# A hybrid block with routed experts: w1 in chunks of contiguous rows, gate and up computed chunk by chunk

## The chip, the core and the metric

The kernel runs on one core of a Trainium2 chip. The metric is the device time in microseconds of one execution; lower is better. Three runs of the kernel before stand beside one profiled execution of it. An engine's "row" below is a line of the profile or of an answer of its trace.

## What is computed

The input is `x` of 256 tokens by 1024 features, all in fp32. A first block does adaptive modulation, a mixer (dilated attention beside a gated delta rule) and a routed mixture of experts; two layers of a second block follow. The change touches the mixture of experts alone:

```python
N_EXPERTS, TOP_K, D_EXPERT, SWIGLU_LIMIT, SWIGLU_ALPHA = 32, 4, 1024, 7.0, 1.702

def clamped_swiglu(hgu):
    gate, up = jnp.split(hgu, 2, axis=-1)
    gate = jnp.minimum(gate, SWIGLU_LIMIT)
    up = jnp.clip(up, -SWIGLU_LIMIT, SWIGLU_LIMIT)
    return gate * jax.nn.sigmoid(SWIGLU_ALPHA * gate) * (up + 1)

h = modulate(x, norm2_w, shift2, scale2)      # rms_norm(x)*w*(1+scale)+shift
logits = h @ w_router + b_router              # top 4 of 32, softmax over the four
# for the tokens xb of expert e:
y = clamped_swiglu(xb @ w1[e] + b1[e]) @ w2[e] + b2[e]
# w1[e]: 1024 x 2048 (gate and up columns), w2[e]: 1024 x 1024
```

## The kernel before, in words

The program writes out each engine's order by hand. TensorE multiplies, VectorE and ScalarE work on what it leaves in the eight banks of its accumulator memory, GpSimd does little, and the sync engine (SP) issues nearly all transfers. Every step waits on counted semaphores.

**Expert pass.** Each expert is given 64 slots for tokens; tokens beyond 64 go to overflow blocks, of which this input has one. So there are 33 passes of one kind. A pass on TensorE is `step` (L1185): `up` (L1142), then `scatter` of the expert before, `gather` of the next one's tokens (L1122), `turn` (L1156, transposes of the activation), `gates` of the next, `down` (L1162). The token matrix of an expert is held as `xe`, features on partitions: 8 blocks of 128 features by 64 tokens. `halves` (L1135) issues one product of 64 tokens by 1024 columns as two matmuls of 512 columns into the lower and the upper 64 partitions of a bank; in fp32 each shows as two instructions in the trace. So one block of 128 weight rows by 1024 columns is four matmul rows of the profile.

`up` fills the gate bank GB and then the up bank UB. Each begins with the bias, a product of the expert's one-hot row (32 partitions) with the table of all biases (4 matmuls with K=32 in the trace), and goes on with 8 feature blocks (32 matmuls). Then VectorE runs `swiglu_v` (L962): clamp both, multiply, add one to the exponential that ScalarE made (L1040), reciprocal (L971), product (L973). The product is what `turn` waits for. `aT` holds its four transposes, and `down` multiplies them with w2.

**Weights.** The ring has six slots of 16 KB per partition. `expert_chunk` (L1231) cuts an expert into six chunks of 2 MB, one per slot. Chunks 0 and 1 are the gate columns of w1, feature rows 0 to 511 and 512 to 1023; 2 and 3 are the up columns; 4 and 5 are w2. Partition p of a chunk holds rows p, 128+p, 256+p and 384+p, each a contiguous run of 4 KB in the device's memory. In `later_sync` (L1240) the sync engine loops over experts 1 to 31: for each chunk it waits until its slot is free (`readers`, L1258: gate_f twice, up_f twice, y_f twice, the ends of gate, up and down of the expert before) and issues the transfer (L1268). Ahead of this loop it writes a table of relative-position rows to the device's memory (L1249) and reads it back (L1257). Expert 0 is loaded earlier, the overflow block by L1277.

**Modulation.** `modulate` (L394) computes h from x for both uses: per tile of 128 tokens one scale instruction over 1024 features (L401) and one shift instruction (L404). The second use stands ahead of the router (L898). `to_features` transposes h, the router matmul (L1074) uses the transposed h and the router weights `wrt`, and `gather` takes its columns from h in every pass.

## Time and profile before

| | |
|---|---|
| Device time, median of 3 runs | 2606.88 us |
| lowest and highest | 2591.89 and 2608.11 us |
| Span of the profiled execution, first to last instruction (the page gives no time of its own beside it) | 2597.9 us |
| TensorE busy | 2358.2 us, 91% |
| VectorE busy | 837.0 us, 32% |
| ScalarE busy | 333.9 us, 13% |
| Moved by the DMA engines | 603.41 MB, mean 232 GB/s |
| Mean granted TensorE clock | 0.931 of 2.4 GHz |

PE is TensorE's matmul stream, PEld its weight loads, DVE VectorE, ACT ScalarE, POOL GpSimd, SP the sync engine and SPq its DMA queue. The span is cut into 40 equal slices of 65 us in the page, where a digit is the busy share of a slice in tenths. `PEclk` is the clock that TensorE was granted, in tenths of the full 2.4 GHz; the lower level is 1.2 GHz. In a group of instructions the columns are busy time and the mean of one; behind the bar stands the idle time of the engine before them and what ended it.

### The profile page before, as it was taken

The numbers are of one execution on the slowest core, as the hardware profiler recorded it, in microseconds if no ns is written. First come the engines' busy times: TensorE is split into PE (matmuls) and PEld (weight loads), VectorE is DVE, ScalarE is ACT, GpSimd is POOL, SyncE is SP. The second block draws the span as 40 slices with busy tenths as digits, with TensorE's granted clock in tenths as the row PEclk, the third lists the DMA queues.
The fourth block names the chain that finished last, engine by engine and source line by source line (L and its number), as shares of the span: only waits on it lengthen the run. The fifth ranks groups of instructions, "written<-read, shape, count | busy, mean of one in ns | idle before, by whom it ended". The sixth has DMA issues, their size and how long they took to land.

```text
span 2597.9 us, 25146 instructions
## 1 busy us (share of the span) xinstructions
PE 2358.2 (91%) x10045; PEld 1253.4 (48%) x10045; DVE 837.0 (32%) x1274; ACT 333.9 (13%) x707; POOL 44.4 (2%) x25
## 2 busy tenths in 40 slices
PE   4988788999999999999999759989899899988999
PEld 2856442333333333333333235454786454546874
DVE  1454321222222222122222215551463045423550
ACT  1132100000000000000000011220221012211110
POOL 0001000000000000000000000000000001000000
PEclk8999878999898999999999869999999999989999
DMA  9463239999899999999999643423443333224431
GB/s 364 147 232 130 79 47 409 392 369 373 354 382 380 364 363 364 371 371 362 365 364 373 256 139 130 146 99 97 130 162 146 115 126 141 97 65 130 156 140 61
DMA packets 219468, 603.41 MB, mean 232 GB/s; under 512 B 10142, under 2 KB 66478, under 8 KB 219234
## 3 DMA queue, kind: packets, MB, share of 16 engines
q1 hardware_dynamic: 219394, 602.40, 62.1%
q8 instruction: 50, 0.82, 0.1%
q14 instruction: 24, 0.20, 0.0%
HBM read 599.23 MB, written 3.15 MB: 232 GB/s over the span
## 4 chain that ended last, share of the span: by engine, by line
issue 61%; PE 33%; DVE 3%; ACT 1%; POOL 1%; SPq 1%; DMA 1%; DVEq 0%; POOLq 0%
PE bank L560 16%; PE bank L568 7%; PE bank L1927 6%; PE bank L767 2%; PE bank L2158 1%; PE bank L552 1%; DMA normw<-in_norm_w_dram 1%; POOL arena L1443 0%; PE bank L434 0%; SPq L1962 0%; PE bank L1834 0%; DVE hbuf L1572 0%; DVE arena L1573 0%; DVE arena L2015 0%; DVE normw L2043 0%
## 5 line engine op out<-in xcount | busy, mean ns | idle before, releaser
L1138 PE MATMUL bank<-ring,arena 128*64 128x512 f32 x3168 | 760.1, 636 | 9.8 <-DMA ring<-in_w_dram 9.8
L1138 PEld LDWEIGHTS bank<-ring,arena 128*64 128x64 f32 x3168 | 231.8, 146 | 545.5 <-issue 532.3
L560 PE MATMUL bank<-hTbuf,ring 128*128 128x256 f32 x1856 | 405.7, 382 | 4.2 <-ACT hTbuf L1680 3.5
L560 PEld LDWEIGHTS bank<-hTbuf,ring 128*128 128x128 f32 x1856 | 355.0, 192 | 54.2 <-issue 5.5
L964 DVE TENSOR_SCALAR arena<-bank 128x512 f32<-128x512 f32 x33 | 22.8, 691 | 519.9 <-PE bank L1138 519.9
L1927 PE MATMUL bank<-ring 128*128 128x512 f32 x352 | 151.4, 592 | 0.0
L568 PE MATMUL bank<-ring,hTbuf 128*128 128x512 f32 (+2 forms) x384 | 151.2, 554 | 0.0
L1125 PEld LDWEIGHTS bank<-arena,hbuf 128*128 128x128 f32 x1056 | 123.8, 196 | 24.7 <-issue 24.6
L1138 PE MATMUL bank<-arena 32*64 32x512 f32 x396 | 121.7, 694 | 14.0 <-ACT arena L1044 14.0
L1125 PE MATMUL bank<-arena,hbuf 128*128 128x64 f32 x1056 | 128.0, 281 | 0.0
L957 DVE TENSOR_SCALAR arena<-con,arena 128x64 f32<-128x64 f32 x66 | 16.5, 250 | 320.7 <-PE bank L1138 307.0
L1642 DVE SCALAR_TENSOR_TENSOR arena<-bank,arena 128x254 f32<-128x254 f32 (+1 forms) x176 | 76.6, 477 | 127.7 <-ACT arena L1773 126.2
L1844 PE MATMUL bank<-ring,hTbuf 128*128 128x512 f32 x256 | 115.3, 604 | 0.0
L971 DVE RECIPROCAL arena<-arena 128x512 f32<-128x512 f32 x33 | 110.7, 3353 | 1.1
L568 PEld LDWEIGHTS bank<-ring,hTbuf 128*128 128x128 f32 x384 | 72.6, 190 | 75.1 <-issue 71.8
L1927 PEld LDWEIGHTS bank<-ring 128*128 128x128 f32 x352 | 66.9, 190 | 83.3 <-issue 83.2
L568 PE MATMUL bank<-ring,arena 128*128 128x512 f32 (+1 forms) x208 | 94.4, 614 | 10.0 <-ACT arena L1680 9.2
L1040 ACT ACTIVATE arena<-arena 128x512 f32<-128x512 f32 x33 | 20.8, 629 | 552.5 <-DVE arena L964 552.5
L552 PE MATMUL bank<-con,hbuf 128*128 128x128 f32 x128 | 25.7, 384 | 61.7 <-DVE hbuf L1457 41.0
L1844 PEld LDWEIGHTS bank<-ring,hTbuf 128*128 128x128 f32 x256 | 48.2, 193 | 62.5 <-issue 62.3
L1654 DVE RECIPROCAL arena<-arena 128x512 f32<-128x512 f32 x22 | 73.8, 3353 | 0.7
L1773 ACT ACTIVATE arena<-bank,arena 128x256 f32<-128x256 f32 x88 | 44.9, 560 | 212.8 <-PE bank L560 212.8
(342 smaller groups left out, 1705.7 us busy)
## 6 DMA issues: line engine op xcount, KB each, us to landing
ring<-in_w_dram SPq DMA_DIRECT2D x198, 2048.0 KB, 12.8
ring<-in_w_up_dram SPq DMA_DIRECT2D x44, 1024.0 KB, 6.5
ring<-in_w_in_dram SPq DMA_DIRECT2D x21, 2048.0 KB, 8.1
ring<-in_w_ada_dram SPq DMA_DIRECT2D x12, 2048.0 KB, 8.2
ring<-in_w_down_dram SPq DMA_DIRECT2D x10, 2048.0 KB, 7.7
ring<-in_w_out_dram SPq DMA_DIRECT2D x6, 2048.0 KB, 8.0
ring<-in_w_in_dram SPq DMA_DIRECT2D x4, 1024.0 KB, 13.4
ring<-in_w_proj_a_dram SPq DMA_DIRECT2D x2, 2048.0 KB, 7.9
```

The source lines that it names most:

```text
L552: ins = pe.transpose(B.bank(name, j)[:, at:at + P], src(k, tt), ident)
L560: ins = pe.matmul(B.bank(name, j)[:, i * T:(i + 1) * T], w[:, k, (first + i) * P:(first + i + 1) * P], hT[:, k, :], start=(k == 0), stop=( ...
L568: ins = pe.matmul(B.bank(name, j)[:, 0:width], xs(k), ws(k), start=(k == 0), stop=(k == kts - 1))
L767: return lambda out, u: pe.matmul(out, lhsT[:, u, :], rhs[:, u, :], start=True, stop=True)
L971: v.reciprocal(eb, eb).then_inc(F["s1"], 1)
L1125: ins = pe.matmul(XB[:, k * SLOTS:(k + 1) * SLOTS], h[:, tt, k * P:(k + 1) * P], psel[:, tt, :], start=(tt == 0), stop=(tt == 1))
L1138: ins = pe.matmul(bank[g * SLOTS:(g + 1) * SLOTS, :], lhsT, rhs[:, g * CH:(g + 1) * CH], start=start, stop=stop)
L1642: ins = v.scalar_tensor_tensor(out=y2[:, k, back:], in0=pb[:, k, 0:T - back], scalar=conv_cols[:, 44 * (2 - back) + m:44 * (2 - back) + m ...
L1654: then(v.reciprocal(fe[i % 2], fe[i % 2]))
L1773: ins = act.activation(split(y, 2)[:, k, :], pb[:, k, :], ACT.Identity, scale=conv_cols[:, 88 + m:89 + m], bias=conv_cols[:, 132 + m:133 + m])
L1844: pe.matmul(BL.bank(f"g{i}", tt)[:], hT[:, k, tt * P:(tt + 1) * P], w[:, k, :], start=(k == 0), stop=False)
L1927: ins = pe.matmul(BL.bank("dn", j)[:], actT[:, k, tt * P:(tt + 1) * P], w[:, k - 4 * i, half * CH:(half + 1) * CH], start=(k == 0), stop=( ...
```

## The change

Chunks 0 to 3 of an expert are now 256 whole rows of w1 each, gate and up columns together, and partition p of a chunk holds rows 2p and 2p+1, one contiguous run of 16 KB. The w2 chunks hold rows 4p to 4p+3 per partition, also 16 KB. To match, `modulate` in its second use writes h with the features of each group of 256 dealt in two: even ones first, then odd ones, four instructions of 256 features where one of 1024 was. The router weights are loaded in the same feature order. The activation product L973 reads its two inputs at every fourth column and writes contiguously, so that the transposes have the features on the partitions where the new w2 chunks expect them. `up` issues both biases first and then goes chunk by chunk: two feature blocks into the gate bank, the same two into the up bank. Three new semaphores c0, c1, c2 tell the sync engine that a chunk has been read; the fourth chunk is let go with `up_f`. The number of matmuls, their shapes and the bytes moved stay as they were.

```diff
--- before.py
+++ after.py
@@ -244,7 +244,7 @@
 MFLAGS = [
     "sel", "x_f", "xe",
     "pgt_f", "pgt",
-    "gate_f", "up_f",
+    "c0", "c1", "c2", "gate_f", "up_f",
     "g_in", "gu_out",
     "g_exp", "s1", "act",
     "at_f", "aT",
@@ -391,17 +391,30 @@
         def bview(b, n):
             return b[:].rearrange("p (a b) -> p a b", a=n)
 
-        def modulate(v, then, sh, nw, job, count):
+        def dealt(row):
+
+            return [row[:, 2 * P * c:2 * P * (c + 1)].rearrange("p (q k) -> p k q", k=2) for c in range(4)]
+
+        def held(row):
+            return [split(row[:, 2 * P * c:2 * P * (c + 1)], 2) for c in range(4)]
+
+        def whole(row):
+            return [row]
+
+        def modulate(v, then, sh, nw, job, count, deal=whole, held=whole):
 
             shift, scale = mod[:, 3 * sh * D:(3 * sh + 1) * D], mod[:, (3 * sh + 1) * D:(3 * sh + 2) * D]
             v.wait_ge(*B.taken(*job))
             then(v.scalar_tensor_tensor(out=scale, in0=scale, scalar=1.0, in1=normw[nw][:], op0=ALU.add, op1=ALU.mult))
             v.wait_ge(S["rs"], count)
             for tt in range(TT):
-                then(v.scalar_tensor_tensor(out=h[:, tt, :], in0=x[:, tt, :], scalar=rs[:, tt:tt + 1], in1=scale,
-                                            op0=ALU.mult, op1=ALU.mult))
+                for hp, xp, sp_ in zip(held(h[:, tt, :]), deal(x[:, tt, :]), deal(scale)):
+                    ins = v.scalar_tensor_tensor(out=hp, in0=xp, scalar=rs[:, tt:tt + 1], in1=sp_, op0=ALU.mult, op1=ALU.mult)
+                then(ins)
             for tt in range(TT):
-                v.tensor_tensor(h[:, tt, :], h[:, tt, :], shift, ALU.add).then_inc(S["h_new"], 1)
+                for hp, sp_ in zip(held(h[:, tt, :]), deal(shift)):
+                    ins = v.tensor_tensor(hp, hp, sp_, ALU.add)
+                ins.then_inc(S["h_new"], 1)
 
         def head(place):
 
@@ -895,7 +908,7 @@
             ins.then_inc(S["x_new"], 1)
             v.wait_ge(S["ss"], 2)
             v.tensor_scalar(ms, ss, 1.0 / D, EPS, ALU.mult, ALU.add).then_inc(S["ms"], 1)
-            modulate(v, then, 1, 1, ("ad2", 3), 2)
+            modulate(v, then, 1, 1, ("ad2", 3), 2, dealt, held)
 
             v.wait_ge(*B.ready("rt"))
             v.tensor_tensor(lg, split(B.bank("rt")[:, 0:2 * NE], 2), brt.unsqueeze(1).to_broadcast([P, 2, NE]), ALU.add)\
@@ -970,7 +983,8 @@
             v.wait_ge(F["s1"], 2 * n + 1)
             v.reciprocal(eb, eb).then_inc(F["s1"], 1)
             v.wait_ge(F["s1"], 2 * n + 2)
-            v.tensor_tensor(act_b, ub, eb, ALU.mult).then_inc(F["act"], 1)
+            v.tensor_tensor(act_b.rearrange("p (q a) -> p q a", q=4), ub.rearrange("p (a q) -> p q a", q=4),
+                            eb.rearrange("p (a q) -> p q a", q=4), ALU.mult).then_inc(F["act"], 1)
 
         def pgt_v(v, F, n, par):
             v.wait_ge(F["pgt_f"], n + 1)
@@ -1113,11 +1127,11 @@
 
             def weights(i, ch):
                 s = (N1 + ch) % RING
-                return slot(s).rearrange("p (k n) -> p k n", k=4), (slot_in[s], 16 * (per_slot[s] + 1) + 16 * i)
+                return split(slot(s), 2 if ch < 4 else 4), (slot_in[s], 16 * (per_slot[s] + 1) + 16 * i)
 
             def over_weights(j, ch):
                 s = (N1 + ch) % RING
-                return slot(s).rearrange("p (k n) -> p k n", k=4), (over_in[s], 16 + 16 * j)
+                return split(slot(s), 2 if ch < 4 else 4), (over_in[s], 16 + 16 * j)
 
             def gather(F, n):
                 for k in range(KT):
@@ -1144,14 +1158,18 @@
                 pe.wait_ge(F["sel"], n + 1)
                 if not (isinstance(n, int) and n == 0):
                     pe.wait_ge(F["gu_out"], n)
-                for m, (bank, flag) in enumerate(((GB, "gate_f"), (UB, "up_f"))):
+                for m, bank in enumerate((GB, UB)):
                     halves(bank, bsel[par], b12[:, m * D:(m + 1) * D], True, False)
-                    for a in range(2):
-                        w, landed = wts(i, 2 * m + a)
-                        pe.wait_ge(*landed)
-                        for k in range(4):
-                            ins = halves(bank, xe[:, 4 * a + k, :], w[:, k, :], False, a == 1 and k == 3)
-                    ins.then_inc(F[flag], 1)
+                for ch in range(4):
+                    w, landed = wts(i, ch)
+                    pe.wait_ge(*landed)
+                    for m, bank in enumerate((GB, UB)):
+                        for k in range(2):
+                            ins = halves(bank, xe[:, 2 * ch + k, :], w[:, k, m * D:(m + 1) * D], False, ch == 3 and k == 1)
+                        if ch == 3:
+                            ins.then_inc(F[("gate_f", "up_f")[m]], 1)
+                    if ch < 3:
+                        ins.then_inc(F[f"c{ch}"], 1)
 
             def turn(F, n):
                 pe.wait_ge(F["act"], n + 1)
@@ -1230,12 +1248,9 @@
 
         def expert_chunk(e, ch):
 
-            rows = slice((ch % 2) * CH, (ch % 2 + 1) * CH)
             if ch < 4:
-                src = A["w1"][0, e, rows, (ch // 2) * D:(ch // 2 + 1) * D]
-            else:
-                src = A["w2"][0, e, rows, :]
-            return src.rearrange("(k p) n -> p k n", p=P)
+                return A["w1"][0, e, 2 * P * ch:2 * P * (ch + 1), :].rearrange("(p k) n -> p (k n)", p=P)
+            return A["w2"][0, e, CH * (ch - 4):CH * (ch - 3), :].rearrange("(p k) n -> p (k n)", p=P)
 
         def later_sync(sp):
 
@@ -1255,11 +1270,11 @@
                     at = qt * 8 * P + odd * 4 * nk
                     src = bass.AP(scratch.tensor, odd * REL + T - 1 - P * qt, [[8 * REL - 1, P], [2 * REL, 4], [1, nk]])
                     sp.dma_start(split(biasbuf[:, at:at + 4 * nk], 4), src).then_inc(S["rel_in"], 16)
-            readers = ["gate_f", "gate_f", "up_f", "up_f", "y_f", "y_f"]
+            readers = ["c0", "c1", "c2", "up_f", "y_f", "y_f"]
 
             def views(ch):
                 s = (N1 + ch) % RING
-                return s, slot(s).rearrange("p (k n) -> p k n", k=4)
+                return s, slot(s)
 
             with sp.Fori(1, NE) as e:
                 for ch in range(RING):
@@ -1952,7 +1967,8 @@
                                        (alog, A["A_log"][0].partition_broadcast(P)),
                                        (dtb, A["dt_bias"][0].partition_broadcast(P)),
                                        (dnw, A["dn_norm_w"][0].partition_broadcast(P)),
-                                       (wrt, A["w_router"][0].rearrange("(k p) n -> p k n", p=P)),
+                                       (wrt.rearrange("p (c k) n -> p c (k n)", c=4),
+                                        A["w_router"][0].rearrange("(c p k) n -> p c (k n)", c=4, p=P)),
                                        (brt, A["b_router"][0].partition_broadcast(P)),
                                        (thin[0:32, 0:8], A["rel_bias_2"])):
                         sp.dma_start(dst2, src2).then_inc(S["small_in"], 16)
@@ -1964,7 +1980,7 @@
             for ch in range(RING):
                 n = N1 + ch
                 sp.wait_ge(*B.ready(*loads1[n - RING][2]))
-                sp.dma_start(slot(n % RING).rearrange("p (k n) -> p k n", k=4), expert_chunk(0, ch))\
+                sp.dma_start(slot(n % RING), expert_chunk(0, ch))\
                   .then_inc(slot_in[n % RING], 16)
             later_sync(sp)
 
```

## Rows read from the trace of the kernel before

**Rows 1.** From the page: span, busy share, and slices of TensorE, its clock and DMA.

```profile
span 2597.9 us, 25146 instructions
...
PE 2358.2 (91%) x10045; PEld 1253.4 (48%) x10045; DVE 837.0 (32%) x1274; ACT 333.9 (13%) x707; POOL 44.4 (2%) x25
...
PE   4988788999999999999999759989899899988999
...
PEclk8999878999898999999999869999999999989999
DMA  9463239999899999999999643423443333224431
```

**Rows 2.** Waits in the expert stage: who for whom, us in total, times, longest.

```profile
PE bank L1159 <- DVE arena L973: 42.2, 32, 6.7
...
PE bank L1138 <- DMA ring<-in_w_dram: 9.8, 3, 7.9
...
SPq L1268 <- PE bank L1138: 869.2, 85, 18.3
```

**Rows 3.** Windows, one pass each: length, busy by engine, PEclk, DMA share, GB/s.

```profile
521.95:554.05 32.10, 30.61 (x156) 12.18 (x154) 7.80 (x13) 2.42 (x4) 0.00 (x0) 1.00 0.99 390
554.05:589.51 35.46, 33.96 (x156) 12.80 (x154) 7.82 (x13) 2.42 (x5) 0.00 (x0) 0.90 0.90 355
589.51:624.53 35.02, 33.73 (x156) 12.90 (x154) 7.80 (x13) 2.42 (x5) 0.00 (x0) 0.90 0.92 360
727.11:760.92 33.81, 32.32 (x156) 12.58 (x154) 7.81 (x13) 2.42 (x4) 0.00 (x0) 0.95 0.95 373
897.31:932.19 34.88, 33.59 (x156) 13.12 (x154) 7.80 (x13) 2.42 (x5) 0.00 (x0) 0.90 0.91 360
932.19:965.99 33.80, 32.31 (x156) 12.53 (x154) 7.81 (x13) 2.42 (x5) 0.00 (x0) 0.95 0.95 372
```

**Rows 4.** Window over thirty passes, from the second exponential to the thirty-second.

```profile
417.67:1443.57 1025.90, 982.92 (x4622) 380.71 (x4620) 233.18 (x356) 72.61 (x120) 0.00 (x0) 0.93 0.94 372
```

**Rows 5.** Timeline of TensorE in one full-clock pass: start, us, what, idle before.

```profile
615.66 1.07 PE L1138 MATMUL bank<-arena 32*64 32x512 f32 x4
616.67 7.09 PE L1138 MATMUL bank<-ring,arena 128*64 128x512 f32 x32
623.68 1.99 PE L1177 MATMUL bank<-arena 64*128 64x512 f32 x8
625.60 3.79 PE L1125 MATMUL bank<-arena,hbuf 128*128 128x64 f32 x32
630.41 0.63 PE L1159 MATMUL bank<-con,arena 128*128 128x128 f32 x4 [1.03 <-DVE arena L973]
```

**Rows 6.** Timeline of VectorE in the same pass.

```profile
625.12 0.69 DVE L967 SCALAR_TENSOR_TENSOR arena<-arena 128x512 f32<-128x512 f32 x1
...
629.58 0.69 DVE L973 TENSOR_TENSOR arena<-arena 128x512 f32<-128x512 f32 x1
```

**Rows 7.** DMA in 618 to 638 us (expert chunks), in 25 to 29 us (constants).

```profile
DMA packets 2079, 8.25 MB, mean 413 GB/s; under 512 B 64, under 2 KB 64, under 8 KB 2079
...
DMA packets 216, 1.79 MB, mean 447 GB/s; under 512 B 16, under 2 KB 16, under 8 KB 93
```

**Rows 8.** Timeline of TensorE in expert 1.

```profile
397.88 8.77 PE L1138 MATMUL bank<-ring,arena 128*64 128x512 f32 x32 [7.92 <-DMA ring<-in_w_dram]
...
413.24 3.65 PE L1138 MATMUL bank<-ring,arena 128*64 128x512 f32 x16 [1.47 <-DMA ring<-in_w_dram]
```

**Rows 9.** Modulation before the router (timeline), and two-input instructions of 256 (groups).

```profile
315.51 1.28 DVE L401 SCALAR_TENSOR_TENSOR hbuf<-x,small,arena 128x1024 f32<-128x1024 f32 x1
316.83 2.36 DVE L404 TENSOR_TENSOR hbuf<-hbuf,arena 128x1024 f32<-128x1024 f32 x2
319.25 1.11 PE L552 MATMUL bank<-con,hbuf 128*128 128x128 f32 x4 [10.73 <-DVE hbuf L404]
...
L1492 DVE SCALAR_TENSOR_TENSOR arena<-arena 128x256 f32<-128x256 f32 x14 | 6.8, 485 | 0.7
```

**Rows 10.** Timeline of TensorE in the pass of 35.46 us: down, then gate.

```profile
562.85 9.84 PE L1138 MATMUL bank<-ring,arena 128*64 128x512 f32 x32
...
573.62 7.09 PE L1138 MATMUL bank<-ring,arena 128*64 128x512 f32 x32
```

## The prediction, made before the result was known

> **What bounds the kernel now.** I read the page's forty slices first [rows 1]. From slice 6 to 22 TensorE and the DMA engines are both at nine tenths: this is the expert stage, 33 passes (32 experts and one overflow block), where nearly the whole change lies. Two resources that full can't both be the bound, so the next view is the list of waits inside the stage [rows 2]. TensorE waited for weights three times, 9.8 us in all, while the sync queue waited 869.2 us for TensorE to let go of a ring slot. So the weights come early and TensorE sets the pace. Its one regular wait is the transpose at L1159, which waits 42.2 us in 32 times for the activation product at L973.
>
> The windows cut at the exponentials of successive experts [rows 3] show one pass. With the clock granted in full (1.00, 2.4 GHz) it takes 32.10 us; others take 33.80, 34.88, 35.02 and 35.46 at 0.95 or 0.90, which means that part of them ran at 1.2 GHz. Thirty passes took 1025.90 us, 34.20 each [rows 4]. So 2.1 us of every pass are clock. The last column matters too: at 32.10 us the transfers are at 0.99 of their capacity and 390 GB/s. The cover over the DMA is thin.
>
> The order inside a full-clock pass is in the rows of TensorE [rows 5] and VectorE [rows 6]: four bias matmuls, 32 with weights (gate), four bias, 32 (up), scatter of the expert before, gather of the next, a gap of 1.03 us, transposes, down. The gap ends when L973 ends.
>
> **The change, part by part.**
> (a) *Bias matmuls together, gate and up chunk by chunk.* The count of matmuls stays: 8 with K=32 and 64 with weights. What changes is how often TensorE goes from one kind to the other. From start to start, 4 bias matmuls take 616.67 - 615.66 = 1.01 us and 32 weight matmuls 623.68 - 616.67 = 7.01 us [rows 5]. With a pace u per matmul and an extra w per change of kind, 4u + w = 1.01 and 32u + w = 7.01, so u = 0.214 and w = 0.153 us. Two changes of kind fall away per pass: 2 x 0.153 = 0.31 us. New is that the accumulation goes between two banks, seven times more per pass. The scatter, 8 matmuls over four banks, takes 1.92 us against 8u + w = 1.87 [rows 5], so three bank changes cost at most 0.05 us; seven cost at most 0.12. I take 0.31 saved (bounds 0.19 and 0.31; zero if w belongs to the start of an accumulation and not to the change of kind). Over 33 passes: **-10.2 us**. All of it is on the path, since VectorE starts its chain only when the last up matmul is done.
>
> (b) *Three chunks released singly.* c0 is let go after about a quarter of the up work instead of half, c2 at three quarters instead of the end; c1 and the last chunk about where they were. The queue behind SP's wait is only the next chunks, and nobody on TensorE waits for them [rows 2]. Price 0, hidden by the lead of the transfers. If that cover were gone, the release would help.
>
> (c) *16 KB per partition.* 512 pieces of 4 KB become 128 of 16 KB per chunk. In a stretch of nothing but 4 KB pieces the queue moved 413 GB/s [rows 7]. The nearest row for larger ones is the start, where the constants come as 13 KB per partition: 447 GB/s over 4 us, a short window and so a rough figure. The gain is between none and 8 per cent of the transfer time, and it counts only where TensorE waits: expert 1, whose chunks are asked for late, behind the bias rows. There the last one gates the last 16 up matmuls at 413.24, 15.4 us after the first at 397.88 [rows 8]. I take 0.5 us (bounds 0 and 1.2): **-0.5**. That new weights come in the order in which they are used changes nothing here, since the last chunk still gates the end.
>
> (d) *The activation product with a stride.* L973 now reads both inputs at every fourth float. It lasts 0.69 us for 512 floats [rows 6] and TensorE waits for its end, so anything added counts in full, 33 times. No DVE row of this trace reads with such a stride. Below: 0, the same number of elements. Above: as if each float were fetched twice, the price of a two-input instruction of 1024, 2.36 / 2 = 1.18 us [rows 9], so +0.49 us, or +16 over all passes. I take 0, by the nearest row in size, type and place: L967 in the same pass, two fp32 inputs of 512, 0.69 us [rows 6]. I hold this loosely.
> The Trainium skill speaks against me: "SBUF — State Buffer", section "Door 1: The DMA port swizzle", says that memory is read in lines of 16 bytes, that full rate wants at least two hits on a line, and that each access which goes to a new line pays. Every fourth float is one hit per line. By that rule (d) costs about the upper bound, and the total comes out slower; no row here shows it. The stride of two in (e) keeps two hits.
>
> (e) *Modulation in four pieces.* Before routing, two scale instructions of 1.28 us and two shift instructions of 1.18 become four each of 256 floats; TensorE waits for the last of them at 319.25 [rows 9]. A two-input instruction of 256 lasts 0.485 us [rows 9]: 2 x (1.94 - 1.28) + 2 x (1.94 - 1.18) = +2.8 at most; as such instructions start before their predecessor's record ends, I take **+2.0**. Once.
>
> (f) Router weights in pieces of 256 bytes instead of 128, at the start, behind larger loads: 0.
>
> **Sum** with the clock as before: -10.2 - 0.5 + 2.0 = -8.7 us. The profiled span is 2597.9 us [rows 1], 9.0 below the median 2606.9 and inside the runs' 2591.9 to 2608.1; span after about 2589, and I apply the difference to the median: **2598 us**.
>
> **The rivals.**
> *R1, the strided product costs.* Place: L973, price up to 0.49 us a pass. It decides from 0.26 us on (8.7 / 33): above that the kernel is slower than before. With the full price and the clock as before: -8.7 + 16.2 = +7.5, 2614 us. The longer trough before down is where the clock falls: in the pass of 35.46 us the 32 weight matmuls of down take 9.84 us, in the gate behind it 7.09 again [rows 10]. If no pass ran at full clock any more and the mean were 35.02 instead of 34.20, 31 x 0.8 = 25 more (without the first and the last pass): 2640 us. For it: nothing hides behind L973. Against it: no row.
>
> *R2, the clock gives it back.* Three different sequences of passes come to one mean: 32.10, 35.46, 35.02 to 34.19; with a 33.81 added to 34.10; 34.88, 33.80, 33.81 to 34.16 [rows 3]. The 32.10 is paid for by the 35.46 behind it. It looks as if the clock's stretches set the mean and not the sum of the work, and then 0.31 us saved turn into a longer stretch at 1.2 GHz. Result: -0.5 + 2.0 + a little, 2608 us, no change.
>
> *R3, the clock gives more.* The same shift may go the other way: the pass is shorter by 0.31 us and more of the troughs go by at full clock. If the mean came to 33.6 instead of 34.20: 31 x 0.6 = 19, with (e): 2589 us; if to 33.3, 2580.
>
> *R4, the DMA becomes the bound.* A pass moves 6 x 2.1 = 12.6 MB; at 34.20 us that is 368 GB/s. If 16 KB pieces ran 20 per cent below 413 [rows 7], at 330 GB/s, a pass would take 38.1 us: 31 x 3.9 = +121, 2728 us. It decides from 11 per cent down. Against it: the 13 KB pieces are not slower. That the change doesn't do what it says (the pieces still move as 4 KB) only takes away the 0.5 of (c).
>
> **Chances.** Forecast (0.31 kept, product free) 0.35; R2 0.20; R3 0.15; R1 0.25, of which 0.10 with the clock lost too; R4 0.05. The sign is thus open between small numbers; what lies outside 1 per cent (26 us, about what a measurement of this kernel tells from no change) is R3's far end, 0.10, and R1 with the clock or R4, 0.15. Range: 2578 (R3 with a little more) to 2636 (R1 with most of its clock). The forecast's own range is 2588 to 2606.
>
> **What would show it.** Step (a): from the first bias matmul to the scatter 15.7 us at full clock instead of 16.0 (2 x 1.01 + 2 x 7.01). (d): the duration of the product, 0.69 or 1.2, and the gap before the transposes, 1.0 or 1.5. (c): no wait of TensorE for weights after expert 1, and the rate in a stretch of expert loads at 413 or above. (e): 2 us more between the mean squares and the first transposes. R2, R3: the mean of thirty passes, 34.2 against 33.9 (forecast) or below, and how many are at clock 1.00. The prediction is wrong if the product lasts over 0.95 us, if a full-clock pass isn't 31.8 us, or if the mean pass moves by over 0.6 us while the full-clock pass doesn't.

## The result, and the profile after

The changed kernel takes 2619.62 us (median of 10 runs, 2612.44 to 2624.59) against 2607.35 us before (10 runs, 2591.89 to 2612.46): ratio 1.0055, 95% interval 1.0035 to 1.0075. It is a little slower. The prediction had it a little faster, 2598 us; the range of 2578 to 2636 holds the measured time, the direction was wrong.

The page of the changed kernel: the head, sections 1 and 2.

```profile
span 2612.7 us, 25156 instructions
...
PE 2362.8 (90%) x10043; PEld 1269.3 (49%) x10045; DVE 850.6 (33%) x1286; ACT 334.1 (13%) x707; POOL 44.4 (2%) x25
...
PEclk9989868899999999989999869989999999989999
DMA  9463239888888998888888543423443334224431
```

Beside [rows 1] the slices of DMA in the expert stage went from 9 to 8: the same bytes with less time of the engines. VectorE is busy for 13.6 us more. TensorE's clock has one nine less, 30 instead of 31, and one of the lost ones stands behind the experts (the 27th slice).

The waits of TensorE and of the sync queue in 380 to 1510 us, as in [rows 2]:

```profile
PE bank L1177 <- DVE arena L986: 54.1, 32, 7.0
...
PE bank L1152 <- DMA ring<-in_w_dram: 6.8, 3, 4.4
```

```profile
SPq L1283 <- PE bank L1152: 942.1, 151, 20.2
```

The wait for the product (L986 now, L973 before) grew from 42.2 to 54.1 us in 32 times, which is the 0.37 us of the next rows. They stand in a pass of the changed kernel whose trough ran at full clock, TensorE and then VectorE, to be laid beside [rows 5, 6]:

```profile
592.37 3.79 PE L1139 MATMUL bank<-arena,hbuf 128*128 128x64 f32 x32
597.56 0.63 PE L1177 MATMUL bank<-con,arena 128*128 128x128 f32 x4 [1.40 <-DVE arena L986]
...
608.59 1.93 PE L1152 MATMUL bank<-arena 32*64 32x512 f32 x8
```

```profile
L986 DVE TENSOR_TENSOR arena<-arena 128x512 f32<-128x512 f32 x33 | 35.1, 1064 | 1.1
```

The same group in the kernel before:

```profile
L973 DVE TENSOR_TENSOR arena<-arena 128x512 f32<-128x512 f32 x33 | 22.8, 692 | 1.1
```

The product lasts 1.06 us where it lasted 0.69, and the gap before the transposes is 1.40 us where it was 1.03. The reader should see the two 0.37 us as one: nothing hides behind this instruction. The eight bias matmuls now stand together and take 1.86 us to the next start.

Windows of the changed kernel: thirty passes, then three kinds of pass (columns as in [rows 3]).

```profile
418.21:1448.20 1029.99, 976.26 (x4622) 387.50 (x4620) 244.41 (x356) 72.62 (x120) 0.00 (x0) 0.93 0.89 370
557.41:591.30 33.89, 32.02 (x156) 12.76 (x154) 8.19 (x13) 2.42 (x5) 0.00 (x0) 0.95 0.89 371
625.18:660.02 34.84, 33.18 (x156) 13.23 (x154) 8.17 (x13) 2.42 (x4) 0.00 (x0) 0.90 0.87 361
1069.15:1105.57 36.42, 34.76 (x156) 13.58 (x154) 8.18 (x13) 2.42 (x4) 0.00 (x0) 0.86 0.83 346
```

No pass of the thirty ran at full clock; before, four of them did, at 32.1 us as the first of [rows 3]. There is a new kind at clock 0.86, 36.42 us. The mean is 34.33 us against 34.20 [rows 4]. So the expert stage lost little in this execution. More went behind it, where no instruction was changed. From the last exponential of the stage to the end, before and after:

```profile
1487.56:1687.56 200.00, 160.80 (x532) 88.08 (x532) 82.51 (x163) 37.50 (x86) 13.25 (x5) 0.88 0.39 133
1687.56:1851.56 164.00, 144.26 (x528) 85.83 (x527) 59.91 (x60) 32.20 (x87) 0.69 (x1) 0.95 0.32 106
1851.56:2597.90 746.34, 704.97 (x2560) 468.12 (x2558) 304.79 (x457) 117.20 (x262) 13.24 (x5) 0.96 0.36 122
```

```profile
1493.76:2612.70 1118.94, 1017.79 (x3615) 648.62 (x3616) 447.58 (x678) 187.05 (x435) 27.19 (x11) 0.94 0.35 121
```

The three windows of before add up to 1110.34 us; the one of after is 1118.94 us, 8.6 us more, with VectorE and ScalarE as busy as before (447.2 and 447.6 us, 186.9 and 187.1) and TensorE busy 7.8 us longer for the same matmuls: 1017.79 against 1010.04. That is its clock: cut into the same three lengths, the stretch of after has a granted clock of 0.87, 0.90 and 0.96 against 0.88, 0.95 and 0.96, and in the second TensorE gets through 496 matmuls where it did 528.

### The profile page after: what moved, and what is told of

The parts are those of the page before. It is cut to its first block, busy times and chain, and to the rows that moved or that the text cites. A ratio compares the mean times of both kernels' runs of the same rounds, so it can differ in the third digit from the quotient of the medians.

```text
span 2612.7 us, 25156 instructions
## 1 busy us (share of the span) xinstructions
PE 2362.8 (90%) x10043; PEld 1269.3 (49%) x10045; DVE 850.6 (33%) x1286; ACT 334.1 (13%) x707; POOL 44.4 (2%) x25
## 4 chain that ended last, share of the span: by engine, by line
issue 61%; PE 33%; DVE 3%; ACT 1%; DMA 1%; POOL 1%; SPq 0%; DVEq 0%; POOLq 0%
PE bank L573 15%; PE bank L581 7%; PE bank L1942 6%; PE bank L780 2%; PE bank L2174 1%; PE bank L565 1%; DMA ring<-in_w_ada_dram 1%; POOL arena L1458 0%; PE bank L447 0%; PE bank L434 0%; PE bank L1849 0%; DVE hbuf L1587 0%; DVE arena L1588 0%; DVE arena L2031 0%; DVE normw L2059 0%
## 5 line engine op out<-in xcount | busy, mean ns | idle before, releaser
L1152 PE MATMUL bank<-arena 32*64 32x512 f32 x396 | 114.8, 687 | 13.4 <-ACT arena L1058 13.4
L1177 PE MATMUL bank<-con,arena 128*128 128x128 f32 x132 | 26.5, 336 | 57.3 <-DVE arena L986 57.3
```

The costliest lines, as they stand in the source:

```text
L1152: ins = pe.matmul(bank[g * SLOTS:(g + 1) * SLOTS, :], lhsT, rhs[:, g * CH:(g + 1) * CH], start=start, stop=stop)
L1177: ins = pe.transpose(YB[:, q * P:(q + 1) * P], act_b[:, q * P:(q + 1) * P], ident)
```

## The experiments

In all of them a pass is counted from one exponential to the next, and "thirty passes" from the second to the thirty-second, as in [rows 4]. Each ratio is to the kernel before as it ran beside that experiment. The **work of a pass** is the time that it takes with the clock at 1.00 throughout.

### Taking the parts away

**e1: w2 and the product as before, all else as changed.**

```diff
-            v.tensor_tensor(act_b.rearrange("p (q a) -> p q a", q=4), ub.rearrange("p (a q) -> p q a", q=4),
-                            eb.rearrange("p (a q) -> p q a", q=4), ALU.mult).then_inc(F["act"], 1)
+            v.tensor_tensor(act_b, ub, eb, ALU.mult).then_inc(F["act"], 1)
-            return A["w2"][0, e, CH * (ch - 4):CH * (ch - 3), :].rearrange("(p k) n -> p (k n)", p=P)
+            return A["w2"][0, e, CH * (ch - 4):CH * (ch - 3), :].rearrange("(k p) n -> p k n", p=P)
```

> The changed kernel with w2 fetched as before (four 4 KB rows per partition) and the product reading contiguously again; w1 in 16 KB, chunk order, biases first and single releases stay. Theory P (the strided read is what made it slower): the product lasts 0.69 us again instead of 1.07, a full-clock pass takes 31.8 us, and the kernel is no slower than before. If the work saved counts, the mean pass is 33.8 to 33.9 us and the ratio to before 0.995 to 0.997; if the clock sets the mean (theory C), the mean pass stays at 34.1 to 34.2 and the ratio is 1.000. Rival D (the 16 KB pieces or the chunk order cost something): ratio stays at 1.005 with the product at 0.69.

Measured: ratio 0.9996 (0.9976 to 1.0015). The product lasts 0.692 us, six of the thirty passes ran at full clock in 31.81 us, and the mean is 33.70:

```profile
L986 DVE TENSOR_TENSOR arena<-arena 128x512 f32<-128x512 f32 x33 | 22.8, 692 | 1.1
```

```profile
418.82:1429.80 1010.98, 968.44 (x4622) 386.45 (x4620) 233.22 (x356) 72.61 (x120) 0.00 (x0) 0.94 0.92 377
1474.58:2586.51 1111.93, 1011.20 (x3616) 642.41 (x3616) 447.15 (x678) 186.96 (x435) 27.19 (x11) 0.95 0.36 121
```

Rival D falls: w1 in 16 KB runs, the chunk order and the single releases cost nothing that shows. What made the changed kernel slower came in with w2's layout and its product. This run takes both back at once, and no run has w2 in 16 KB runs with a contiguous product; but in the changed kernel TensorE never waits for weights after expert 1 (420 to 1450 us), so w2's loads are not what it waits for. The two readings of the clock are not told apart by this run: the profiled execution has the lower mean of theory W, the median of the runs gained nothing. That execution, at 2588.7 us, was one of the quickest of the twelve. What became of the saved work shows when the twelve are laid beside their granted clocks ("The clock over the kernels" below).

**e2: the kernel before, both biases first, nothing else.**

```diff
-                for m, (bank, flag) in enumerate(((GB, "gate_f"), (UB, "up_f"))):
+                for m, bank in enumerate((GB, UB)):
                     halves(bank, bsel[par], b12[:, m * D:(m + 1) * D], True, False)
+                for m, (bank, flag) in enumerate(((GB, "gate_f"), (UB, "up_f"))):
```

> The kernel before with one edit: both biases ahead of the gate matmuls. Full-clock pass 31.8 us instead of 32.1 if the 0.15 us per change of kind is real (32.1 if it belongs to the start of an accumulation). Theory W (work counts): mean pass 33.9, ratio 0.996. Theory C (the clock gives it back): mean pass 34.1 to 34.2, ratio 1.000, and another mixture of passes.

Measured: ratio 0.9972 (0.9945 to 0.9999). TensorE in a pass at full clock, and the windows of thirty passes and of one such pass:

```profile
908.68 1.93 PE L1138 MATMUL bank<-arena 32*64 32x512 f32 x8
910.54 13.95 PE L1138 MATMUL bank<-ring,arena 128*64 128x512 f32 x64
924.43 1.99 PE L1178 MATMUL bank<-arena 64*128 64x512 f32 x8
```

```profile
420.33:1432.86 1012.53, 969.98 (x4622) 386.23 (x4620) 233.15 (x356) 72.62 (x121) 0.00 (x0) 0.94 0.96 376
960.42:992.23 31.81, 30.31 (x156) 12.35 (x154) 7.81 (x13) 2.42 (x4) 0.00 (x0) 1.00 1.00 394
```

From the first bias matmul to the scatter 924.43 - 908.68 = 15.75 us, where the kernel before takes 2 x (623.68 - 615.66) = 16.04 [rows 5]. The 0.15 us per change of kind are real. In this profile the mean pass fell by more than the work, from 34.20 to 33.75 us, but the stretch behind the experts took 1119.0 us instead of 1110.3. Over all executions the median fell by 5.3 us (2594.07 against 2599.37) where 33 x 0.30 = 9.9 us of work were saved, and the interval of the ratio just excludes no change. So the work counts here, but the clock didn't give more than was saved.

**e3: the kernel before, with w2 in 16 KB runs and the strided product.**

```diff
-            v.tensor_tensor(act_b, ub, eb, ALU.mult).then_inc(F["act"], 1)
+            v.tensor_tensor(act_b.rearrange("p (q a) -> p q a", q=4), ub.rearrange("p (a q) -> p q a", q=4),
+                            eb.rearrange("p (a q) -> p q a", q=4), ALU.mult).then_inc(F["act"], 1)
-                src = A["w2"][0, e, rows, :]
+                return A["w2"][0, e, rows, :].rearrange("(p k) n -> p (k n)", p=P)
```

> The kernel before with w2 in 16 KB runs and the strided product; gate and up as before. Theory P: product 1.07 us, gap before the transposes 1.4 us, a full-clock pass would be 32.5 us. If work counts: mean pass 34.6, ratio 1.005. If the longer gap also costs clock: no pass at full clock, mean 34.9 or more, ratio 1.008 or more. If the clock alone sets the mean: 34.2, ratio 1.000.

Measured: ratio 1.0003 (0.9979 to 1.0026). The product lasts 1.07 us as in the changed kernel, and yet the time doesn't change:

```profile
L973 DVE TENSOR_TENSOR arena<-arena 128x512 f32<-128x512 f32 x33 | 35.2, 1067 | 1.1
```

```profile
416.87:1442.17 1025.30, 969.41 (x4622) 375.99 (x4620) 244.47 (x356) 72.60 (x120) 0.00 (x0) 0.95 0.93 371
1486.20:2589.50 1103.30, 1002.38 (x3616) 634.97 (x3616) 447.50 (x678) 186.86 (x435) 27.19 (x11) 0.96 0.36 122
930.17:964.31 34.14, 32.27 (x156) 12.52 (x154) 8.19 (x13) 2.42 (x5) 0.00 (x0) 0.95 0.93 368
```

Every pass of the thirty but the first took 34.1 to 34.2 us, all at clock 0.95, and the thirty are 34.18 in the mean, where 0.37 us more work on 34.20 would be 34.6. This is rival R2 with its sign turned: 0.37 us of work were added and the clock gave them back. The product isn't free here: the twelve executions had a mean granted clock of 0.938 where the kernel before had 0.931, and at one clock e3 is the slower of the two ("The clock over the kernels").

**e4: the changed kernel, reading contiguously and writing with the stride.**

```diff
-            v.tensor_tensor(act_b.rearrange("p (q a) -> p q a", q=4), ub.rearrange("p (a q) -> p q a", q=4),
-                            eb.rearrange("p (a q) -> p q a", q=4), ALU.mult).then_inc(F["act"], 1)
+            v.tensor_tensor(act_b.rearrange("p (q a) -> p a q", q=4), ub.rearrange("p (a q) -> p a q", q=4),
+                            eb.rearrange("p (a q) -> p a q", q=4), ALU.mult).then_inc(F["act"], 1)
```

> The changed kernel, but the product reads contiguously and writes with the stride (each next float 512 bytes on). If only reads by lines cost, the product lasts 0.69 us and this equals e1 in time with all weights in 16 KB runs. If a strided write costs as a strided read, 1.07 us and ratio 1.005 to before; if each write of a new line costs more, over 1.2 us and ratio 1.01.

Measured: ratio 1.0041 (1.0019 to 1.0063); the product lasts 1.041 us.

```profile
L986 DVE TENSOR_TENSOR arena<-arena 128x512 f32<-128x512 f32 x33 | 34.4, 1041 | 1.1
```

A strided write costs nearly what a strided read costs. There is no free side to put this stride on.

**i1: one strided input instead of two** (the other is read contiguously, so its columns no longer match and the activation is another one).

```diff
-            v.tensor_tensor(act_b.rearrange("p (q a) -> p q a", q=4), ub.rearrange("p (a q) -> p q a", q=4),
+            v.tensor_tensor(act_b.rearrange("p (q a) -> p q a", q=4), split(ub, 4),
                             eb.rearrange("p (a q) -> p q a", q=4), ALU.mult).then_inc(F["act"], 1)
```

> The changed kernel, the product reading only the exponential's input with the stride and the other contiguously (the columns then don't match, so the activation is another one). Both inputs strided took 1.07 us, none 0.69. If the cost is per strided stream and they add up: 0.88. If one strided stream already sets the pace of the instruction: 1.07.

Measured in its one execution: 1.070 us, as with two.

```profile
L986 DVE TENSOR_TENSOR arena<-arena 128x512 f32<-128x512 f32 x33 | 35.3, 1070 | 1.1
```

One strided stream sets the pace of the instruction. What in the stride costs is not shown: no run gives this instruction a stride of two or three floats.

**i2: the changed kernel, slots released in pairs.**

```diff
-            readers = ["c0", "c1", "c2", "up_f", "y_f", "y_f"]
+            readers = ["c1", "c1", "up_f", "up_f", "y_f", "y_f"]
```

> The changed kernel with the slots of w1 released in pairs again: chunks 0 and 1 after the second chunk, 2 and 3 at the end of up. Everything else as changed. Forecast step (b) priced the single release at nothing: ratio 1.005 as the changed kernel, no wait for weights after expert 1. If the single release had a price or a use: ratio off by more than 0.003 from the changed kernel's.

Measured: ratio 1.0094 (1.0068 to 1.0120), 0.0039 above the changed kernel's first ratio and 0.0046 above its second (g0 below), whose intervals it meets only at the edge. Yet in 420 to 1450 us TensorE waited for weights once, 1.2 us, and its thirty passes took 1040.60 us, 34.69 each, inside what the changed kernel itself shows (34.33 and 34.78). By the mark set above, a change of over 0.003, the release has a use. But it isn't a wait for weights, and at one granted clock i2 takes what the changed kernel takes ("The clock over the kernels"): its executions ran at a lower clock, 0.9205 in the mean against 0.9224. Why they did stays open.

### What repeats and what does not

**g0: the changed kernel once more**, unedited.

> The changed kernel once more, to see what repeats. Up to the last exponential of the expert stage it is 6 us behind the kernel before, and another 8.5 us are lost behind the expert stage, where no instruction was changed (1118.8 instead of 1110.3 us), in stretches at 1.2 GHz around the attention of the first layer. Theory H (the expert stage hands the layers a fixed place in the clock's rhythm): the stretch behind the last exponential is again 1118 to 1119 us. Rival N (chance of the single execution): it is anywhere between 1103 and 1119.

Measured: ratio 1.0048 (1.0027 to 1.0070).

```profile
420.00:1463.50 1043.50, 990.95 (x4622) 390.90 (x4620) 244.48 (x356) 72.63 (x121) 0.00 (x0) 0.91 0.88 365
1509.10:2628.10 1119.00, 1017.93 (x3615) 648.36 (x3616) 447.62 (x679) 187.05 (x435) 27.19 (x11) 0.94 0.35 121
```

The thirty passes are 13.5 us longer than in the first profile, with five passes at 36.4 us instead of one; the stretch behind them is the same to 0.1 us. This profile is of the slowest of g0's ten executions, 2630.31 us where their median is 2615.98.

**h0: the kernel before once more**, unedited.

> The kernel before once more, for a second profile of it. Theory H (the expert stage hands the layers a place in the clock's rhythm, and in the changed kernel always the same bad one): behind the last exponential 1110 us again or another value below 1118. Rival N: 1118 to 1119 is seen here too. The thirty passes should come to 34.1 to 34.3 us each.

Measured: one run, 2589.93 us.

```profile
417.50:1439.70 1022.20, 978.76 (x4622) 378.55 (x4620) 233.28 (x357) 72.66 (x121) 0.00 (x0) 0.94 0.95 373
1483.90:2588.10 1104.20, 1003.32 (x3615) 636.56 (x3616) 447.28 (x678) 186.98 (x435) 27.19 (x11) 0.96 0.36 122
```

Thirty passes at 34.07, and 1104.20 us behind them. Before thus shows 1110.3 and 1104.2 us there, the changed kernel 1118.9 and 1119.0 (and i2 1118.8). e2, which has neither the strided product nor a larger run, shows 1119.0 too; e3 shows 1103.3. The other kernels lie between: f4, f6 and e4 at 1118.7 to 1119.0, i1 at 1116.4, f3 at 1115.7, e1 at 1111.9. So the two profiles of the changed kernel lose 9 to 15 us there, but the loss is not peculiar to one of its parts, and i1, which differs from it in one input of the product, shows 2.5 us less. That it hangs on how the expert stage leaves TensorE's clock is the likely reading and isn't shown. Nor is the place fixed for the kernel before: 69 of its executions have spans from 2585.9 to 2613.5 us, and 20 of the changed kernel from 2605.2 to 2628.1.

**g1: the changed kernel with an idle instruction between the experts and the layers.**

```diff
+            then(v.reciprocal(t[:, 0:256], t[:, 0:256]))
             for tt in range(TT):
...
```

> The changed kernel with one idle reciprocal of 256 columns (1.7 us) on the path between the experts and the layers. It adds 1.7 us of work. Theory H: the layers start at another place in the clock's rhythm, the stretch from the last exponential to the end falls from 1118.8 to about 1105 to 1112 in spite of the added work, and the median is 5 to 10 us lower than the changed kernel's (ratio to before 0.999 to 1.003). Rival N: 1.7 us slower than the changed kernel, ratio 1.006.

Measured: ratio 1.0060 (1.0037 to 1.0083). In the profile the last stretch fell as theory H has it, in spite of the 1.7 us added:

```profile
1497.17:2609.89 1112.72, 1009.82 (x3615) 643.59 (x3616) 449.33 (x679) 187.20 (x435) 27.21 (x11) 0.95 0.36 121
```

The median did not fall. Either the other five executions left the experts at another place, or the gain was lost elsewhere; only one was profiled. Theory H is borne out by one profile, and the gain in time that it foretold did not come.

### Filling the gap

In the changed kernel TensorE idles 1.40 us behind each gather. The bias matmuls of the next expert need nothing that isn't there by then: both banks have been read by the clamps. The edit moves them, for three bases.

```diff
                 if more:
                     gather(M, i + 1)
+                if more:
+                    biases(M, i + 1, 1 - par)
                 if not first:
                     pe.wait_ge(M["ysb"], i)
                 turn(M, i)
```

**f4: on the changed kernel.**

> The changed kernel with the two biases of the next expert issued in the gap before the transposes (behind the gather), all weights in 16 KB runs, strided product. TensorE's gap of 1.4 us is filled, the pass at full clock would be 30.9 us. With the gap filled the strided product (1.07 us) costs nothing. If work counts: mean pass 31.5 to 32.9, 1.3 to 2.7 us less than 34.2, ratio 0.970 to 0.985. If the transfers become the bound: 12.6 MB a pass at 431 GB/s is 29.2 us, so not with 16 KB runs. If the clock alone sets the mean: 34.1, ratio 1.00.

**f3: on e1** (contiguous product).

> As the one before, but w2 in four 4 KB rows and the product contiguous (0.69 us). The bias matmuls fill the gap either way, so the strided product should make no difference: full-clock pass 30.9 us as well. Against the one before it tells the product on the path (no difference expected) from the transfers: w2 at 413 GB/s instead of 431 makes a pass of transfers 29.7 us, still below 30.9, so the same time within 0.1 per cent; slower if the DMA is now the bound.

**f6: on the kernel before.**

> The kernel before (weights in 4 KB rows, gate then up, contiguous product) with the two biases of the next expert issued in the gap behind the gather, and nothing else. It tells what the change itself is worth once the gap is filled. If the gain of the two gap kernels (0.981 and 0.987) is all from the filled gap: full-clock pass 30.6 us, no wait for weights, ratio 0.981 to 0.987. If the transfers at 4 KB now bind (12.6 MB at 413 GB/s is 30.5 us, at the full-clock pass's edge): waits of TensorE for the ring in several passes, ratio 0.99.

Measured: f4 0.9814 (0.9785 to 0.9843), f3 0.9865 (0.9831 to 0.9899), f6 0.9853 (0.9810 to 0.9895). The passes of TensorE in f4 between gather and down, and thirty passes of f4, f3 and f6:

```profile
913.78 3.79 PE L1139 MATMUL bank<-arena,hbuf 128*128 128x64 f32 x32
917.50 1.93 PE L1152 MATMUL bank<-arena 32*64 32x512 f32 x8
919.36 0.66 PE L1179 MATMUL bank<-con,arena 128*128 128x128 f32 x4
```

```profile
418.19:1404.02 985.83, 972.61 (x4622) 383.81 (x4620) 245.34 (x356) 72.61 (x121) 0.00 (x0) 0.93 0.93 386
```

```profile
420.27:1401.06 980.79, 967.58 (x4622) 383.10 (x4620) 233.25 (x356) 72.63 (x121) 0.00 (x0) 0.93 0.95 387
```

```profile
421.41:1396.50 975.09, 960.01 (x4622) 381.73 (x4620) 233.18 (x356) 72.63 (x121) 0.00 (x0) 0.94 0.99 390
```

The gap is gone, and in f4 nothing in 420 to 1340 us waits for the product, though it lasts 1.09 us there. All three have a full-clock pass of 30.59 us, 0.3 less than was expected of f4 and f3, for a reason not looked into. f4 is 1.9 per cent faster than the kernel before; but the three intervals overlap, so what the change adds once the gap is filled can't be told from nothing. f3 and f4 were to be equal within 0.1 per cent and are 0.5 apart. Their mean granted clocks are 0.925 and 0.930, and at one clock they meet: at 0.923 f3 has one execution of 2567.1 us, f4 two of 2564.0 and 2568.2. As to the transfers, f6 has 4 KB runs and the DMA engines at 0.99 of their time. TensorE waited for weights four times in 370 to 1450 us, 13.6 us in all; all but one wait of 1.4 us lie before 420 us, at expert 1, as ever.

### The clock over the kernels

| kernel | work of a pass | mean of thirty | lost to the clock |
|---|---|---|---|
| f6, f3, f4 | 30.59 | 32.50, 32.69, 32.86 | 1.9, 2.1, 2.3 |
| e1, e2 | 31.81 | 33.70, 33.75 | 1.9, 1.9 |
| before, h0 | 32.11 | 34.20, 34.07 | 2.1, 2.0 |
| changed, g0, g1, i2, i1 | 32.18 (worked out) | 34.33, 34.78, 34.38, 34.69, 34.66 | 2.2 to 2.6 |
| e4 | 32.16 (worked out) | 34.11 | 2.0 |
| e3 | 32.48 (worked out) | 34.18 | 1.7 |

Where no pass ran at full clock the work is worked out as 32.11, less 0.30 where the biases stand together, plus what the product takes beyond 0.69. The loss is no constant: 1.7 to 2.6 us, largest in the changed kernel and smallest in e3, which has the most work.

That table rests on one profile for each name. Every execution, profiled or not, also has a span and a mean granted clock of its own, and these let the kernels be compared at one clock. "Before" is here the 69 executions that ran beside the experiments, "changed" the ten of the result and the ten of g0.

| kernel | executions, their mean clock | those at 0.924 to 0.927, mean span |
|---|---|---|
| before | 69, 0.9315 | 11, 2610.0 us |
| changed | 20, 0.9224 | 7, 2610.6 us |
| i2 | 10, 0.9205 | 3, 2611.4 us |
| e4 | 12, 0.9250 | 10, 2607.4 us |
| e1 | 12, 0.9263 | 8, 2596.0 us |
| e2 | 12, 0.9294 | 4, 2596.6 us |
| f6 | 6, 0.9260 | 4, 2559.4 us |
| f3 | 6, 0.9250 | 2, 2559.9 us |

None of e3 or f4 fell into that stretch of clocks. At 0.933 to 0.936 there are 24 of before with a mean of 2591.8 us, 5 of e3 with 2604.8, and 2 of f4 with 2543.8 beside one of f6 with 2544.3. Within the kernel before, a clock 0.001 lower goes with a span about 1.9 us longer (an estimate from its ends, 2586.0 us at 0.938 and 2612.0 at 0.924), so differences of 2 or 3 us in the table mean nothing. Larger ones do:

- e3 is 13.0 us slower than the kernel before at one clock, where 33 x 0.37 = 12.3 us of work were added. That its median equals the other's is the clock.
- The changed kernel is 14.6 us slower than e1, some 2 us of which are that e1's eight have a clock 0.001 higher. The product is worth 12.3.
- e1 and e2 are 13 to 14 us faster than the kernel before (some 12 with their slightly higher clocks allowed for), for 9 to 10 us of work saved. That their medians gained 0.6 and 5.3 us is the clock.
- The changed kernel and the kernel before can't be told apart at one clock. What separates their medians is mostly that the one is granted 0.9224 and the other 0.9315.

The clock of an execution is read after the fact. The table parts work from clock; it doesn't say why one kernel is granted less than another, and no run here does.

## Why the prediction was wrong, point by point

- **(d), the strided product, is the first step that failed.** It was priced at 0 between bounds of 0 and +0.49 us a pass; it takes 0.37, 12.3 us over 33 passes. The nearest row that I chose, L967, was like it in size and type and not in the one thing that changed. The bounds held, the choice in them did not, and rival R1 with the point from which it decides (0.26 us) was the case that came. The prediction's own sign of being wrong, a product over 0.95 us, was met too. The rule of the Trainium skill in "SBUF — State Buffer", section "Door 1: The DMA port swizzle", spoke for it: by it each access that goes to a new line of 16 bytes pays. The runs agree in direction. They give the price as well, a factor of 1.54 on the instruction (1064 / 692 ns) for one strided input as for two and 1.50 for a strided write; e1, e4 and i1 show it. That the line is the reason is not shown by them.
- **(a), biases together, was right.** 15.75 instead of 16.04 us in e2, 0.29 against the forecast 0.31; the full-clock pass is 31.81. The bank changes cost nothing that shows: e1 goes from bank to bank chunk by chunk, e2 doesn't, and both have 31.81.
- **(b), single releases, was priced at 0.** Without them (i2) one wait of 1.2 us shows. i2 is 0.4 per cent slower than the changed kernel by the ratios and not slower at one clock, so the price in work of 0 stands.
- **(c), 16 KB runs.** A stretch of nothing but expert loads, 618 to 638 us, ran at 431 GB/s against 413 [rows 7]:

```profile
DMA packets 590, 8.62 MB, mean 431 GB/s; under 512 B 64, under 2 KB 64, under 8 KB 64
```

  At expert 1 the chunks gate TensorE at these two places (timeline of the changed kernel), 14.7 us apart instead of 15.4 [rows 8]: 0.7 us against the forecast 0.5.

```profile
399.10 8.63 PE L1152 MATMUL bank<-ring,arena 128*64 128x512 f32 x32 [4.37 <-DMA ring<-in_w_dram]
...
413.79 3.65 PE L1152 MATMUL bank<-ring,arena 128*64 128x512 f32 x16 [1.24 <-DMA ring<-in_w_dram]
```

- **(e), modulation in four pieces.** Eight instructions each, in the changed kernel:

```profile
311.95 3.38 DVE L412 SCALAR_TENSOR_TENSOR hbuf<-x,small,arena 128x256 f32<-128x256 f32 x8 [0.67 <-POOL small L2001]
315.37 2.77 DVE L416 TENSOR_TENSOR hbuf<-hbuf,arena 128x256 f32<-128x256 f32 x8
```

  The first starts at 311.95 and TensorE's transposes at 318.20, 6.25 us; before, it was 319.25 [rows 9] less the start of the first scale instruction at 314.19, 5.06. So +1.2 us against the +2.0 taken. A stride of two floats has no price to be seen.
- **The sum, "with the clock as before", is the second step that failed.** With the measured terms: -9.9 + 12.3 - 0.7 + 1.2 = +2.9 us. The medians differ by 12.3. The other 9 us are the clock, which the sum took as unchanged. In the first pair of profiles it is 8.6 us behind the experts (1118.94 against 1110.34) and 2 us in the thirty passes (4.1, less 30 x 0.07 of work); in the second pair 14.8 and 19 us, which is too much for a typical execution, since g0's profile is its slowest run and h0's faster than the median of its kernel. That no work was changed behind the experts is shown. That the rest of the medians' difference is clock is borne out by all executions, which at one clock don't differ; how it splits between the two places is inferred from two profiles a side, and why the clock is granted less is open. Of the 21 us between the forecast of -8.7 and the measured +12.3, (d) is 12.3 and the clock 9; the other terms nearly cancel.
- **The rivals.** R1 was right in the product, and half right in the clock: no pass ran at full clock any more, but the mean was 34.33 and 34.78 us, not 35.02. R2 and R3 are seen on other kernels. R2, the clock undoes a change of work, is e3. R3, it gives more than was saved, is seen only in the thirty passes of the profiles of e1 and e2: 0.30 us less work, 0.50 and 0.45 us less per pass. Their medians gained 0.6 and 5.3 us, less than the 9 to 10 of the work. Neither could be told beforehand from the rows of before, and I didn't put the clock behind the expert stage into any rival. That is what was missing.
- **R4** fell: the larger runs are faster, not slower.

## What to carry to other kernels

A layout that makes a load better has to be paid for where its consumer is put in order; look for that instruction first, and if it stands on the chain that an engine waits for, even a third of a microsecond a pass counts in full, here 12 us over 33 passes. An instruction in the gap of the bound engine costs nothing once the gap is filled with that engine's own later work, and that move (1.9 per cent in f4) was worth more than the whole change either way. Differences of half a per cent in a kernel whose TensorE idles briefly in every pass are decided by the clock as much as by the work: compare several profiles, take the work from passes at one clock, and lay the spans of all executions beside their granted clocks before a ratio of 1.00 is read as "costs nothing".

## What the runs showed of the hardware that I had not expected

- A two-input fp32 product of 512 on VectorE: 692 ns contiguous, 1064 to 1070 ns with one or two inputs at every fourth float, 1041 ns with the output at every 128th float. At every second float and 256 elements, eight in 3.38 us.
- TensorE's granted clock can fall into a fixed beat with the loop: in e3 29 passes in a row took 34.1 to 34.2 us at clock 0.95, with 32.48 us of work by the table's reckoning.
- The same unchanged instructions behind the expert stage took 1103.3 to 1119.0 us in thirteen of the profiles, with VectorE's busy time within 0.6 us; TensorE's busy time went from 1002 to 1019 us.
